# Other order of the first adaptive tiles, the first norm's sums as columns, first scales in PSUM, and a projection that begins unevenly

## The reference

```
sh1, sc1, g1, ... = split(silu(c) @ ada_w[0] + ada_b[0])         # once for c, once for c_ctx
h  = rmsnorm(x, norm1_g[0]) * (1 + sc1) + sh1                    # 256 positions of x, 256 of ctx
rmsnorm(x, g) = x * rsqrt(mean(x * x) + 1e-6) * g
p  = h @ w_in                                                    # gdn_w_in, 32 tiles of 128 columns
...                                                              # convolution, delta rule
y  = (rmsnorm(o, norm_g) * silu(z)) @ w_out                      # gdn_out, 8 tiles
x  = x + g1 * y
```

## Time and profile before

| | us |
|---|---|
| timed, median of 3 | 3640.57 |
| lowest and highest | 3635.67, 3642.06 |
| profiled execution, its time | 3633.79 |
| its span | 3632.5 |
| PE busy in the span | 3406.7 |
| DVE busy | 2777.4 |

### The profile page before, as it was taken

The page is one execution under the profiler, slowest core; times in us unless marked ns, Lnnn a source line. Parts: engine busy times, 40 slices in busy tenths (PEclk is TensorE's granted clock), DMA queues, the critical chain, the costliest instruction groups (busy, mean ns, idle before and its releaser), DMA issues.

```text
span 3632.5 us, 59739 instructions
## 1 busy us (share of the span) xinstructions
PE 3406.7 (94%) x23981; PEld 3182.1 (88%) x23981; DVE 2777.4 (76%) x4937; ACT 1621.9 (45%) x2520; POOL 1517.4 (42%) x820
## 2 busy tenths in 40 slices
PE   7998999999979999799999989999998999988899
PEld 4667998889979999799999977999998999877799
DVE  6867777458999999588888766887755777757585
ACT  3533444333325555333333345546663333458353
POOL 2665555234777787555555300776661000000000
PEclk8999999899989999899999989999999999998899
DMA  6442112323867999989999621577777888631365
GB/s 235 143 124 65 47 53 94 122 87 124 274 203 271 338 336 338 324 310 340 337 336 339 231 88 46 178 219 238 259 263 245 280 278 279 209 118 53 99 198 163
DMA packets 250083, 752.24 MB, mean 207 GB/s; under 512 B 24144, under 2 KB 101840, under 8 KB 242512
## 3 DMA queue, kind: packets, MB, share of 16 engines
q1 hardware_dynamic: 119808, 418.70, 35.9%
q10 hardware_dynamic: 93136, 195.49, 15.3%
q0 software_dynamic: 36864, 134.23, 9.8%
HBM read 661.82 MB, written 85.98 MB: 206 GB/s over the span
## 4 chain that ended last, share of the span: by engine, by line
PE 64%; DVE 15%; DMA 7%; POOL 4%; ACT 4%; issue 4%; ACTq 0%; DVEq 0%; POOLq 0%
PE ps L138 62%; DVE paone L80 3%; POOL lo L80 3%; DMA paGg<-paG 3%; DMA parow<-in_u_rows,paidx 2%; DVE n_sq L113 2%; PE ps L141 2%; DVE paR L80 2%; POOL cond L80 2%; ACT hi L133 1%; DVE lo L80 1%; DVE g_b L80 1%; DVE paav0l L80 1%; DMA paA<-paga 1%; DMA ring<-in_adas 0%
## 5 line engine op out<-in xcount | busy, mean ns | idle before, releaser
L80 POOL TENSOR_TENSOR lo<-ring,hi 128x1024 fp32r<-128x1024 f32 x392 | 956.4, 2445 | 961.4 <-ACT hi L133 960.2
L133 ACT ACTIVATE hi<-ring 128x1024 fp32r<-128x1024 f32 x725 | 768.2, 1060 | 764.1 <-PE ps L138 645.9
L80 DVE TENSOR_TENSOR lo<-ring,hi 128x1024 fp32r<-128x1024 f32 (+1 forms) x333 | 406.7, 1223 | 228.8 <-ACT hi L133 228.1
L138 PE MATMUL ps<-pahh,hi 128*128 128x384 f32 (+1 forms) x1152 | 408.2, 354 | 25.1 <-POOL lo L80 22.2
L138 PE MATMUL ps<-pahl,hi 128*128 128x384 f32 (+1 forms) x1152 | 397.4, 345 | 0.0
L138 PE MATMUL ps<-pahh,lo 128*128 128x384 f32 (+1 forms) x1152 | 397.4, 345 | 0.0
L138 PE MATMUL ps<-pchh,hi 128*128 128x256 f32 x1152 | 334.8, 291 | 14.1 <-POOL lo L80 12.3
L138 PE MATMUL ps<-pchl,hi 128*128 128x256 f32 x1152 | 327.1, 284 | 0.0
L138 PE MATMUL ps<-pchh,lo 128*128 128x256 f32 x1152 | 326.9, 284 | 0.0
L138 PEld LDWEIGHTS ps<-pahh,hi 128*128 128x128 f32 x1152 | 220.7, 192 | 32.7 <-POOL lo L80 24.9
L138 PE MATMUL ps<-g_b,g_b 128*128 128x128 f32 x1856 | 234.5, 280 | 12.8 <-ACT g_b L133 9.3
(11 more groups left out here) (489 smaller groups left out, 9749.5 us busy)
## 6 DMA issues: line engine op xcount, KB each, us to landing
ring<-in_u SPq DMA_DIRECT2D x256, 512.0 KB, 4.2
ring<-in_v SPq DMA_DIRECT2D x256, 512.0 KB, 4.7
ring<-in_adat SPq DMA_DIRECT2D x56, 512.0 KB, 3.6
paA<-paga ACTq DMA_DIRECT2D x128, 192.0 KB, 4.8
paG<-paR ACTq DMA_DIRECT2D x12, 2048.0 KB, 8.5
paAg<-paA ACTq DMA_DIRECT2D x16, 1536.0 KB, 8.6
paGg<-paG ACTq DMA_DIRECT2D x16, 1536.0 KB, 22.7
ring<-in_ffn_up SPq DMA_DIRECT2D x44, 512.0 KB, 3.7
```

What stands on the lines that cost most here:

```text
L80: return Op(self.e.tensor_tensor(out, a, b, op) if self.real else None)
L133: return Op(self.e.activation(out, a, ACT.Copy, scale=scale) if self.real else None)
L138: return Op(self.e.matmul(out, l, r, start=start, stop=stop, skip_group_check=skip) if self.real else None)
```

## The change

It has four parts. The stream's first 16 tiles come in another order of P and D. The first norm sums, takes its root and is spread as all the others do. The 16 sums of the dots and the scale with its bias (`raised`) lie in PSUM bank 5 instead of SBUF. And `proj_pe` takes a list `order` of pairs (block, tile); the first projection gives its own, in which each of the three tiles takes blocks 0 to 3 alone, and blocks 4 to 7 go over all three as before. Without a list the pairs are in the former order, but a tile is now waited for at its first pair, and `ready(c)` is called at every pair.

```diff
@@ -204,7 +204,7 @@
         out.append((("ada", n, q), src.rearrange("(c p) n -> p c n", p=128), 1024, True))
 
     done = {"P": 0, "D": 0}
-    for kind in "PPPPDPDDPDDPDPDD":
+    for kind in "PDPPDPDPDPDPDPDD":
         k = done[kind]
         done[kind] += 1
         if kind == "P":
@@ -472,22 +472,23 @@
         pe.wait_ge(lo_signal(i), i)
         return hi[:, pair_of[i], :], lo[:, pair_of[i], :]
 
-    def proj_pe(tiles, h, a, z, ps, free, ready=None, front=1):
-
-
-
-        ws = [tile(i) for i in tiles[:front]]
-        for n in range(front):
-            free(n)
-        for c in range(8):
+    def proj_pe(tiles, h, a, z, ps, free, ready=None, front=1, order=None):
+
+
+
+        order = order or [(c, n) for c in range(8) for n in range(front)]
+        ws = {}
+        for c, n in order:
             cs = slice(c * 128, (c + 1) * 128)
+            if n not in ws:
+                ws[n] = tile(tiles[n])
+                free(n)
             if ready:
                 ready(c)
-            for n in range(front):
-                op = pe.mm3(ps(n)[:, 0:z - a], (ws[n][0][:, cs], ws[n][1][:, cs]), (h[0][:, c, a:z], h[1][:, c, a:z]),
-                            c == 0, c == 7)
-                if c == 7:
-                    op.then_inc(s_used, tiles[n])
+            op = pe.mm3(ps(n)[:, 0:z - a], (ws[n][0][:, cs], ws[n][1][:, cs]), (h[0][:, c, a:z], h[1][:, c, a:z]),
+                        c == 0, c == 7)
+            if c == 7:
+                op.then_inc(s_used, tiles[n])
         yield front - 1
         for n in range(front, len(tiles)):
             w = tile(tiles[n])
@@ -609,10 +610,7 @@
                              h[0][:, c, lo_ - first:hi_ - first].bitcast(F32), ADD, SUB)
             op.then_inc(s_xn, (name, "low", c))
 
-        if name == "g1":
-            dve.wait_ge(s_rs, name)
-        else:
-            dve.wait_ge(s_sum, (spread or name, "spread"))
+        dve.wait_ge(s_sum, (spread or name, "spread"))
         for c in range(8):
             if c >= 3:
                 dve.wait_ge(s_xn, (name, "low", c - 3))
@@ -674,7 +672,6 @@
     def start(row, junk, dots, first):
 
         s_first, s_table = S("start_dot"), [S(f"crow_loaded{j}") for j in range(2)]
-        s_total, s_root = S("start_sum"), S("start_root")
         for j in range(2):
             act.dma(row[j], d["crow"][:, j, :]).then_inc(s_table[j], 0, 16)
         act.dma(XT[:, :, :], d["xT"]).then_inc(s_x, 0, 16)
@@ -693,25 +690,21 @@
         pe.wait_ge(s_small, 0)
         pe.wait_ge(s_eps, 3)
         pe.wait_ge(s_cond, 0)
-        def total(c):
-
-            if c == 0:
-                pe.wait_ge(s_cst, 0)
-            pe.wait_ge(s_sq, ("g1", c))
-            pe.mm(bank[7][:, :], ones, n_sq[c % 2][:, :], c == 0, c == 7).then_inc(s_sum, ("g1", c))
-
         for t in range(8):
             ada_pe(t // 4, t % 4, 2 + t // 4)
+            if t == 3:
+                pe.wait_ge(s_cst, 0)
             for c in {3: range(0, 4), 4: range(4, 8)}.get(t, ()):
-                total(c)
+                norm_sum("g1", c, 0, 512, 7)
             if t == 5:
                 ada_turn(0, 6, 0)
+            if t == 6:
+                norm_spread("g1", 512)
         ada_turn(1, 6, 8)
         for c in range(8):
             norm_square("g1", c, 0, 512, lambda c: act.wait_ge(s_x, 0))
-        act.wait_ge(s_sum, ("g1", 7))
-        act.act(n_rs[:, :], bank[7][:, :], ACT.Sqrt, bias=eps[:, 0:1], scale=1 / 1024.0).then_inc(s_root, 0)
         ada_evict(0, 2)
+        norm_root("g1", 0, 512, 7)
         ada_evict(1, 3)
         hi_to(at[("gdn_in", 0)])
 
@@ -726,15 +719,18 @@
                 dve.dot(junk[j], slots[slot(i)], row[j], dots[:, 2 * k + j:2 * k + j + 1]).then_inc(s_first, (k, j))
             release[i] = [(s_first, (k, 1))]
             if k == 5:
-                dve.wait_ge(s_root, 0)
-                dve.rcp(bank[SPREAD["g1"]][:, :], n_rs[:, :]).then_inc(s_rs, "g1")
+                norm_inverse("g1", 512)
         dve.wait_ge(s_first, (7, 1))
-        dve.tt(mod[:, 0, 8:16, :], dots[:, :].rearrange("p (n j) -> p n j", j=2),
-               bc(sm("adab0")[:, 8:16].unsqueeze(2), (128, 8, 2)), ADD).then_inc(s_mod, "first")
+        raised = bank[5][:, 0:16].rearrange("p (n j) -> p n j", j=2)
+        dve.tt(raised, dots.rearrange("p (n j) -> p n j", j=2), bc(sm("adab0")[:, 8:16].unsqueeze(2), (128, 8, 2)),
+               ADD).then_inc(s_mod, "first")
         dve.wait_ge(s_col, 1)
         dve.tt(mod[:, 0, 0:8, :], bank[6][:, 0:16].rearrange("p (n j) -> p n j", j=2),
                bc(sm("adab0")[:, 0:8].unsqueeze(2), (128, 8, 2)), ADD).then_inc(s_mod, "shift")
-        ada_scale(0, 0, "first")
+        dve.wait_ge(s_mod, "first")
+        for j in range(2):
+            op = dve.stt(gsc[:, 0, 0, :, j], raised[:, :, j], 1.0, sm("n1g0"), ADD, MUL)
+        op.then_inc(s_mod, (0, 0))
         act.wait_ge(s_mod, "shift")
         dve.wait_ge(s_mod, (0, 0))
         dve.wait_ge(s_cst, 0)
@@ -758,7 +754,7 @@
             qT, kT, vT = (alloc(st, n, [128, 8, 512]) for n in ("g_q", "g_k", "g_v"))
             zT = alloc(st, "g_z", [128, 8, 512])
             crow = [zT[:, 4 + 2 * j:6 + 2 * j, :].rearrange("p a b -> p (a b)") for j in range(2)]
-            start(crow, [qT[:, j, :].bitcast(BF16) for j in range(2)], qT[:, 7, 0:16], qT[:, 7, 16:17])
+            start(crow, [qT[:, j, :].bitcast(BF16) for j in range(2)], bank[5][:, 16:32], qT[:, 7, 16:17])
 
             decay = [alloc(st, "g_g", [128, 4, 16])]
             decay += [n_xn[2][:, 64 * k:64 * k + 64].rearrange("p (a b) -> p a b", a=4) for k in range(8)]
@@ -828,7 +824,8 @@
                     pe.mm(bank[6 + j % 2][:, :], bc(pick[0:40, k:k + 1], (40, 128)), split_inv[j // 8][0:40, :], True,
                           True).then_inc(s_norm, ("spread", j))
 
-                for n in proj_pe(w_in, h, 0, 512, lambda n: bank[n % 4], free, normed("g1"), 3):
+                uneven = [(c, n) for n in range(3) for c in range(4)] + [(c, n) for c in range(4, 8) for n in range(3)]
+                for n in proj_pe(w_in, h, 0, 512, lambda n: bank[n % 4], free, normed("g1"), 3, uneven):
                     if n == AB:
                         pe.wait_ge(s_gate, "wab")
                         for c in range(8):
```

## The result

The changed kernel took 3651.69 us (median of 13 executions, 3634.14 to 3661.24) beside 3638.45 for the kernel before (13 executions): ratio 1.0037, 95% interval 1.0026 to 1.0048. In a second set of six executions, timed later, the ratio was 1.0052 [1.0034, 1.0071]. It is slower by 13 us, and the first measurement lies in the predicted range. How the time came about is another matter: the term for the spreads was right, and the start as it was forecast stood in no profile of this kernel.

The account below looks back on a forecast made before the run. PE carries 64% of the chain that ended last; the start follows a chain of waits. Start 4.0, uneven order 0.3, spreads 7.6 and later tile waits -1.3 sum to +10.6, added to 3638.0: 3649 us, range 3641 to 3656.

Parts of the forecast that it names:

- The spreads: In gdn_out, ready(c) at every pair issues eight more spreads (32 matmuls), 0.93 to 0.96 us each: +7.6 us, nothing hidden.
- Later tile waits: At the projection behind the merge, six matmuls go ahead of the third tile's lo: -1.3 us.
- Start: PE begins the first projection at 55.8 us against 51.77, behind later ada tiles, ACT and POOL: +4.0 us.
- I take this value for the longer part of each group of sums: In the start, one-column sums run at low clock, 1.6 us for eight, and the ada tile behind takes 3.4.
- the second rival: Full clock through the start's sums: tile 6 at 37.6, PE's start at 51.3, total +6.1 us; chance 0.2.
- the last rival: Clock low all through, or several block waits: tile 6 at 45 or later, +14 us, 3653; chance 0.12.
- row of 64 one-column records: Profile row at 666 to 679.5 us: PE busy 13.0 of 13.5 us, granted clock 0.55, used against full clock.
- the forecast's +10.6: The main case for the whole kernel: all four terms together, +10.6 us, 3649; chance 0.48.
- DVE's 9.5 us: Before the first norm, removed reciprocal and waits save DVE 9.5 us, but these stand waiting behind ACT and POOL.
- The third rival: In the start, low(0) does not wait for POOL: PE starts at 52.5 or 47.9, +7.3 or +2.7 us; chance 0.12.
- The not-slower rival: The start's removed waits pay in full: PE starts near 44.9, -6.9 us there, -0.3 in all; chance 0.08.
- Uneven order: In the first projection, PE waits about 0.3 us a block while tile 0 goes alone: +0.3 us, bounds 0 and +2.

Follow-up runs that it names:

- e2: The kernel before with only the new proj_pe (tiles waited for at their first pair, ready(c) at every pair); ratio 1.0015 to the kernel before.
- e1: The changed kernel with ready(c) called once for each block, so gdn_out issues 8 spreads instead of 16; ratio 1.0020 to the kernel before.
- e5: The changed kernel once more, unaltered, for a second profile and timing; ratio 1.0052 to the kernel before.
- e11: The kernel before with only the sums of the dots and the raised scale in PSUM; ratio 1.0010 to the kernel before.
- e7: e1 with the first three projection lo tiles made on DVE in place of POOL; ratio 1.0028 to the kernel before.
- e4: e1 with the first projection taking its three tiles evenly, without the uneven order; ratio 1.0023 to the kernel before.
- e6: e1 with the first norm's sums, root and reciprocal as before (512 columns, no spread); ratio 0.9996 to the kernel before.
- e8: e6 with the old stream order and the first three lo tiles on DVE; ratio 1.0004 to the kernel before.
- e9: e8 with nine useless matmuls in PE's idle time and the first pairs in the order their halves come; ratio 0.9986, repeated unaltered 0.9999.
- e10: The kernel before with thirteen useless matmuls in PE's idle time ahead of the first projection; ratio 0.9993 to the kernel before.

## Why the prediction was right, and where it was not

**The spreads (+7.6)** were right: 7.1 in the changed kernel, 7.15 in e2, nothing in e1. The row-by-row price was 1.80 us a block for two more spreads, 0.90 each and not 0.95.

**Later tile waits (-1.3)**: the wait of 4.19 us became 1.77 at the one place that was named, in the changed kernel and in e2 alike. The size is less sure than it looks: -0.9 and -1.07 at the fourth tile's hi, but -3.4 in e5, whose clock stayed full there, and -1.0 in e11, which has the old `proj_pe` and only a shorter stretch of low clock.

**Start (+4.0)** is the term that was mis-sized. Its working rested on the step "I take this value for the longer part of each group of sums, and 3.4 us for the ada tile behind each". In both profiles of the changed kernel the clock fell for one tile only, tile 6 was used at 38.2, and the start came to -0.3: the second rival's picture (tile 6 at 37.6, first matmul 51.3). In e7, with the same PE instructions up to there, tile 6 was used at 42.1, which is the forecast to the tenth. In e1 and e4 the clock stayed low for some 20 us, tile 6 was used at 47, and the start cost 8.5 and 7.8, past the last rival's "tile 6 at 45 or later". The mechanism that the row of 64 one-column records pointed to is there, but its size differs from one execution to the next: the same PE instructions gave three starts, 9 us apart. What decides it is open; the profiles had parted in clock before the sums began (at 11 to 23 us). The prediction gave these cases separate chances as if one would hold for the kernel, but the start differs from one execution to the next. Timed, the price is 8.7 us (e1 against e6). With e6's start (-1.1), 8.7, 7.1 and -0.9 the sum is +13.8; the two timed sets have +13.5 and +19. That most executions of the changed kernel have the slow start is inferred from this sum, not seen: its two profiles both had the quick one. If it is so, the case that held at the median is the last rival's (+14, chance 0.12) and not the forecast's +10.6, and that 3652 came so near the 3649 of the forecast is in part luck: its start of +4.0 lies between the -0.3 that was profiled and the +7.6 that the times give (-1.1 + 8.7).

**DVE's 9.5 us, hidden behind ACT and POOL**, was right in each part: the order "third hi, then `norm_high`", the low pair that waits for POOL's third lo (4.13 us), and the first matmul right behind. e7 took POOL's part away and got 3.3 us of it. The third rival (the pair does not wait) did not occur in any run where the pair met POOL's lo tiles (2.74 us in e11 to 4.24 in e1, 0.87 alone).

**Not seen at all** was that a gain in front need not arrive. The prediction took each microsecond of PE's first matmul as one of the total. In e8 6.1 us there were 1.1 at hi 4, in e7 3.3 were 0.4, for the most part because PE's clock had fallen while it idled and the first blocks ran at half of it; e9, with the idle time filled and the first pairs reordered, kept 6.7. The not-slower rival (PE starts near 44.9, -6.9) may so have been worth far less than it said; no run had that start with GpSimd's lo tiles, so this is argued and not shown.

**Uneven order (+0.3)**: 0.8 at half clock (e4 against e1), inside its bounds; the timed ratios, 1.0020 and 1.0023, cannot tell.

Behind 760 us the traces drift. Both profiles of the changed kernel stood at some +6.3 near 820 us; the first ended 11.6 us behind before's, the second 3.2 ahead of it. PE's total time at the lower level was 233 us in before, and 248 and 203 in these two. The end of one profile says little of a change in the start; its milestones up to 650 us do, and the medians of many executions.

## What to carry to other kernels

Before adding up waits at a start, look at the granted clock of the work behind them: where the engine idled, the first blocks may run at half speed, and an earlier start may be spent there; filling the idle time tests it. One-column matmuls between dense ones can cost more by the clock of those behind them than by their own time, and differently in each execution, so compare several profiles and the medians. A callback that does work and is made once for a block must not be called once for a pair.

## What the runs showed of the hardware

- Executions with the same instructions at the start were granted different clocks there: the second group of 32 one-column records took 3.63 us in the changed kernel and 6.83 in e1, and PE's clock over 23 to 47 us was 0.90 and 0.57, the second with PE busy throughout.
- Idling pulled the clock down at 39 to 56 us, and 13 matmuls that serve nothing held it at 1.00 (e10).
- In `gdn_out` 40 records of spreads took 6.66 us in before and 7.68 in the changed kernel, at a lower clock; the 1.0 us was hidden, since before had then waited 1.07 us for `h_ol` and the changed kernel did not.
- A pair of low halves beside POOL's three lo tiles took 4.13 us (e11: 2.74) and ended 0.3 us (e11: 0.7) behind the last of them; alone it takes 0.87.
